# Second-block mixing with finer hand-overs and ScalarE making half of the scan's bounded differences

## The chip, the cores and the metric

The kernel runs on one core of one Trainium2 chip, as one launch. Its engines are TensorE (PE, with its weight loads shown apart as PEld), VectorE (DVE), ScalarE (ACT), GpSimd (POOL) and the queue of SyncE (SP), which here only issues DMAs. The metric is the device time of one execution in microseconds, the median of the runs.

## The reference, cut to what matters

All is fp32, 256 tokens (two tiles of 128) of width 1024. A first block has two layers with ffn halves, a state-space scan (layer 0) and pooling (layer 1). A second block has two layers; each mixes (attention, short convolution, spatial gating) and then sums 128 chosen experts per token.

```python
# first block, scan of one chunk of 128 tokens, 32 heads, two directions
seg = a_cum[:, :, :, None] - a_cum[:, :, None, :]
Lmat = jnp.exp(jnp.where(mask, seg, -jnp.inf))
cb = jnp.einsum('bclgn,bcsgn->bclsg', Cc, Bc)
y_diag = jnp.einsum('bclsg,bclsge,bcsgep->bclgep', cb, Lmat, xdt)
y_off = jnp.einsum('bclgn,bcgepn,bclge->bclgep', Cc, h_in, jnp.exp(a_cum))

# second block, one layer
h = rms_norm(x, norm1_g) * (1 + sc1) + sh1
proj = h @ w_in                                # 1024 x 2048
y_attn, y_conv, y_sgu = ...                    # 512, 256 and 256 columns
merged = concatenate([rms_norm(y_attn, ga), rms_norm(y_conv, gc), rms_norm(y_sgu, gs)])
x = x + g1 * (merged @ w_out)                  # 1024 x 1024
h2 = rms_norm(x, norm2_g) * (1 + sc2) + sh2
x = x + g2 * peer_ffn(h2, ...)                 # 8 heads x 16 experts per token; each: dot with a row, gelu, times gate, times a second row, summed
```

## The kernel before, in words

Each engine has a stream of its own, written by hand, and they meet through semaphores. The order of the first block is: `ffn0`, `ffn1`, the scan's projections, the scan, its output projection, `ffn2`, `ffn3`, pooling, `ffn4`. Weights come through a ring of six 1 MB tiles.

**The scan.** 32 batches, each a chunk, a direction and four heads. TensorE makes the running sums of a batch for all positions (`running_sums`, into PSUM bank `BC_BANK[b % 3]`) two batches ahead, and then the outputs of the batch (`outputs`). VectorE (`segments`) subtracts each position's own sum and bounds the difference at zero, four instructions of 128 columns; ScalarE (`exponents`) makes `exp` of the sums (`eoff`) and of the bounded differences (`decay`), 512 columns each; VectorE (`weights`) multiplies by the masked products `cbm`, one batch behind; GpSimd multiplies `eoff`. Between batches VectorE also has `skip`, `weigh_dt`, `gated`, `group_scale` and `group_norm`, and TensorE three `group_sums`; ScalarE has two square roots, each with a change of its table to and back. `decay`, `eoff` and the banks are rings of three, freed by `y_done`, and by `seg_ready` and `expbc_ready`.

**The second block.** Four units `g` (layer, token tile). A unit first mixes and selects its experts, then its 128 picks come: GpSimd gathers a pick's two rows of 1024 for all 128 tokens by an indirect DMA of 1 MB into one of eight slots (`rows`), VectorE makes the dot (L2294), ScalarE gelu, gate and a diagonal matrix (`diag`), and TensorE adds the second row through that diagonal (L625), or VectorE for some picks (L1587). The mixing of unit `g` is a generator (`mix`) on each engine; `mix_slot(g, step)` says before which pick of unit `g - 1` a step is done. For unit 0 all slots of the mixing lie before the first pick, so there it runs by itself, and the picks of unit 0 begin when its first 32 expert numbers (`eidx`) are there. The gathers are in order on GpSimd's queue; the weight tiles of the second block (8 of `w_in`, 4 of `w_out`, 8 of `peer_wq`, 4 small `keys`) come through a ring of four on SP's queue, each reloaded when `weights2_used` says so.

In `mix`, before the change: ScalarE squares and roots (`square_norm`), makes `gd` (eight diagonals of the residual gate `g1` or `g2`), scales the tokens into `xs`. TensorE broadcasts the gate (ones times `gd`, banks 2 and 3), turns `xs` (banks 4 and 5), and ScalarE evicts the eight blocks with norm scale and shift into `u2`, then the gate into `g_b`. Only when all eight blocks are there (`u2_ready`) does TensorE begin `columns`, a tile of 256 columns as eight fp32 matmuls. After attention ScalarE squares the three groups of `merged` (512, 256, 256), one root each, VectorE one reciprocal, ScalarE scales the groups, TensorE turns eight blocks, ScalarE evicts them into `mergedT`, and then four `columns` of `w_out` follow. VectorE waits for all four, multiplies by the gate and adds, 1024 columns each. The second norm goes as the first, and its blocks are turned once more into `h2tok`.

Nearly all instructions of an engine have the line of a helper: L625 is every matmul, L628 every transpose, L1132 every ScalarE activation, L1584 `tensor_tensor`, L1587 `scalar_tensor_tensor`, L1590 `tensor_scalar`, L2427 the gather. `u2` shows as `u`, `decay` as `arena`, `eoff` as `hT` and `xres` as `x_tok`.

## Time and profile before

| what | value |
|---|---|
| median of 3 runs | 3089.16 us (3086.47 to 3093.55) |
| profiled execution | 3088.0 us, span 3085.1 us |
| PE, DVE, ACT, POOL busy | 84%, 71%, 35%, 24% of the span |
| DMA | 977.06 MB, mean 317 GB/s |
| scan | about 691 to 785 us |
| unit 0's mixing | about 1484 to 1615 us |
| picks of four units | 1615 to 3085 us |

A busy share is an average over stages with different limits, so the stages are looked at apart: which wait ends last in each. PE and PEld overlap, and a busy PE isn't PE at its peak. Granted clock 1.00 is 2.4 GHz of TensorE, 0.50 is 1.2 GHz. An instruction's mean is its own duration; the next of the same engine can start before it ends. One profiled execution gives all durations.

### The profile page before, as it was taken

Reading aid. Unit: us, or ns where it says so; the run is one execution under the profiler, and the core shown is the slowest. Engines: PE = TensorE matmul, PEld = TensorE weight load, DVE = VectorE, ACT = ScalarE, POOL = GpSimd, SP = SyncE. Lnnn points to the kernel's source line nnn. Section 1 sums busy time; section 2 is a strip of 40 time slices with the busy share of each in tenths; the row PEclk is TensorE's granted clock in tenths of the full one; section 3 lists DMA queues with packets and bytes.
Section 4 is the critical chain, followed back from the end, with each engine's and each line's share of the span. In section 5 each row is a group of like instructions: output and inputs, shape, how many; then the busy total and the mean of one; then the engine's idle time right before and its main releaser. Section 6 shows DMA issues by size and latency. Waiting matters only on the chain.

```text
span 3085.1 us, 37413 instructions
## 1 busy us (share of the span) xinstructions
PE 2604.5 (84%) x13854; PEld 1978.6 (64%) x13854; DVE 2183.9 (71%) x3896; ACT 1074.0 (35%) x2248; POOL 738.9 (24%) x683
## 2 busy tenths in 40 slices
PE   7999999998999999899876788767786788876656
PEld 5999998886899899899762355324553245532212
DVE  6886866649368878678228766797667966689675
ACT  4434333324243434433322333223432244332221
POOL 0000000005000000000004434344433443344553
PEclk9999999999999999999888898999899998999878
DMA  7766963330369689389449999999999999999997
GB/s 311 266 231 239 369 241 140 112 134 2 130 237 363 258 316 365 138 329 360 161 146 420 409 418 409 420 419 419 421 421 420 411 407 400 420 422 421 421 419 325
DMA packets 137015, 977.06 MB, mean 317 GB/s; under 512 B 15517, under 2 KB 15525, under 8 KB 18992
## 3 DMA queue, kind: packets, MB, share of 16 engines
q0 software_dynamic: 91088, 661.23, 52.7%
q1 hardware_dynamic: 44496, 308.06, 26.2%
q10 hardware_dynamic: 1296, 6.04, 0.5%
q8 instruction: 75, 1.23, 0.2%
q14 instruction: 60, 0.49, 0.0%
HBM read 974.21 MB, written 1.06 MB: 316 GB/s over the span
## 4 chain that ended last, share of the span: by engine, by line
PE 50%; DMA 24%; DVE 14%; issue 5%; ACT 5%; POOL 1%; DVEq 0%; ACTq 0%; POOLq 0%
PE psum L625 49%; DMA rows<-in_peer,eidx 23%; DVE rows L2294 3%; DVE yacc L1587 2%; DVE arena L1732 1%; PE psum L628 1%; ACT L1132 1%; DVE wlow L1584 1%; DVE arena L1584 1%; POOL rows L2427 1%; DVE rep L2083 1%; DVE arena L1590 1%; ACT u L1132 0%; ACT dots L1132 0%; DMA arena<-in_ada_t 0%
## 5 line engine op out<-in xcount | busy, mean ns | idle before, releaser
L625 PE MATMUL psum<-rows,diag 128*128 128x512 f32 x1440 | 791.3, 692 | 347.4 <-ACT diag L1132 340.9
L2294 DVE CUSTOM_DVE_ANT_0 rows<-rows,h2tok 128x1024 f32<-128x1024 f32 x512 | 626.7, 1225 | 334.1 <-DMA rows<-in_peer,eidx 326.2
L2427 POOL DMA_INDIRECT rows<-in_peer,eidx x512 | 618.2, 1207 | 959.6 <-PE psum L625 560.7
L625 PEld LDWEIGHTS psum<-rows,diag 128*128 128x128 f32 x1440 | 292.5, 216 | 777.9 <-ACT diag L1132 493.8
L625 PE MATMUL psum<-u_hi,whigh 128*128 128x256 f32 x1760 | 505.3, 287 | 20.9 <-DVE u_lo L1587 18.1
L625 PE MATMUL psum<-u_lo,whigh 128*128 128x256 f32 x1760 | 501.6, 285 | 0.0
L625 PE MATMUL psum<-u_hi,wlow 128*128 128x256 f32 x1760 | 501.3, 285 | 0.0
L1584 DVE TENSOR_TENSOR wlow<-wring,whigh 128x2048 fp32r<-128x2048 f32 x165 | 377.1, 2289 | 120.9 <-ACT whigh L1132 115.3
L1132 ACT ACTIVATE whigh<-wring 128x2048 fp32r<-128x2048 f32 x165 | 314.1, 1908 | 173.0 <-PE psum L625 132.5
L1132 ACT ACTIVATE dots<-dots 128x2 f32<-128x2 f32 x256 | 52.2, 204 | 891.7 <-DVE dots L2294 891.5
L625 PEld LDWEIGHTS psum<-u_hi,whigh 128*128 128x128 f32 x1760 | 340.8, 194 | 24.1 <-issue 19.3
L625 PEld LDWEIGHTS psum<-u_lo,whigh 128*128 128x128 f32 x1760 | 341.6, 194 | 0.0
L625 PEld LDWEIGHTS psum<-u_hi,wlow 128*128 128x128 f32 x1760 | 341.5, 194 | 0.0
L2388 POOL DMA_DIRECT2D arena<-in_ada_t x112 | 59.5, 532 | 965.5 <-DVE stage L1732 667.4
L1732 DVE CUSTOM_DVE_ANT_0 arena<-arena 128x1024 f32<-128x1024 f32 x224 | 265.5, 1220 | 10.3 <-DMA arena<-in_ada_t 10.3
L625 PE MATMUL psum<-hid_hi,whigh 128*128 128x256 f32 x880 | 250.0, 284 | 3.9 <-DVE wlow L1584 3.9
L625 PE MATMUL psum<-wring,u 128*128 128x256 f32 x1056 | 246.3, 389 | 6.8 <-ACT u L1132 6.8
L625 PE MATMUL psum<-hid_lo,whigh 128*128 128x256 f32 x880 | 249.8, 284 | 0.0
L625 PE MATMUL psum<-hid_hi,wlow 128*128 128x256 f32 x880 | 249.7, 284 | 0.0
L625 PEld LDWEIGHTS psum<-wring,u 128*128 128x128 f32 x1056 | 206.3, 196 | 61.6 <-issue 25.1
L625 PE MATMUL psum<-arena,wring 128*128 128x256 f32 (+1 forms) x912 | 200.5, 380 | 0.0
L1587 DVE SCALAR_TENSOR_TENSOR yacc<-rows,dots,yacc 128x1024 f32<-128x1024 f32 x148 | 189.7, 1282 | 0.0
(274 smaller groups left out, 3231.1 us busy)
## 6 DMA issues: line engine op xcount, KB each, us to landing
arena<-in_ada_t POOLq DMA_DIRECT2D x116, 1024.0 KB, 7.5
wring<-in_ffn_w_gate SPq DMA_DIRECT2D x55, 1024.0 KB, 6.3
wring<-in_ffn_w_up SPq DMA_DIRECT2D x55, 1024.0 KB, 7.1
wring<-in_ffn_w_down SPq DMA_DIRECT2D x55, 1024.0 KB, 6.5
wring<-in_w_in SPq DMA_DIRECT2D x32, 1024.0 KB
wring<-in_peer_wq SPq DMA_DIRECT2D x32, 1024.0 KB
wring<-in_ssd_w_in SPq DMA_DIRECT2D x30, 1024.0 KB, 4.8
wring<-in_w_out SPq DMA_DIRECT2D x16, 1024.0 KB
```

Source lines behind the costliest of these rows:

```text
L625: return nc.tensor.matmul(out, lhsT, rhs, start=start, stop=stop, skip_group_check=shared)
L628: return nc.tensor.transpose(out, in_, ident[0:in_.shape[0], 0:in_.shape[0]])
L1132: return nc.scalar.activation(out, in_, fn, **kw)
L1584: return v.tensor_tensor(out, a, b, op)
L1587: return v.scalar_tensor_tensor(out=out, in0=a, scalar=s, in1=b, op0=op0, op1=op1)
L1590: return v.tensor_scalar(out, a, s1, s2, op0, op1) if op1 is not None else v.tensor_scalar(out, a, s1, None, op0)
L1732: ins = v.tensor_tensor_reduce(out=w, in0=w, in1=crow[:, ADA_VECTOR[n], :], scale=1.0, scalar=0.0, op0=ALU.mult, op1=ALU.add, accum_out=st ...
L2083: ins = v.match_replace(out=spare[:, i, :], in_to_replace=vals[:, i, 0:8], in_values=src[:, i, :], imm_value=-3.0e38)
L2294: v.tensor_tensor_reduce(out=rows[:, n % SLOTS, 0:D], in0=rows[:, n % SLOTS, 0:D], in1=h2tok[:, t, :], scale=1.0, scalar=0.0, op0=ALU.mult ...
L2388: pool.dma_start(aring[:, a % ADA_RING].rearrange("p a b -> p (a b)"), A["ada_t"][it + 4 * (group + a)]) \
L2427: pool.indirect_dma_start(out=rows[:, n % SLOTS, :], out_offset=None, in_=A[f"peer{u // 2}"], in_offset=bass.IndirectOffsetOnAxis(ap=eidx[ ...
```

## The change

It has two parts, in the same functions of the kernel.

- **Scan.** `segments` on VectorE makes the bounded differences of two of a batch's four heads. For the other two ScalarE's `exponents` makes `Relu(-sum + own sum)` from PSUM, which is the bounded difference with its sign turned, and takes its exponent with scale -1. So `decay`'s exponent is two instructions of 256 columns, with a wait for ScalarE's own Relu between.
- **Mixing, all four units.** `xs` is scaled in two halves, each with its count of `xs_ready`. `gd` is made after the eight blocks of `u2`, and the gate's broadcast goes behind tile 1 of `w_in`, into banks 4 and 5, with its own semaphore (`gd_ready`) and `tok_done` back. Each block of `u2` counts, and the first tile and the second transposes wait block by block. In the merge, groups 1 and 2 are squared, rooted, inverted, scaled and turned as soon as they are there (slots 24 to 29), group 0 after attention; the blocks are evicted in `MERGED_ORDER`, each counting, and the first tile of `w_out` takes them in that order. The residual is added in four quarters, each as its tile is done, and the second norm's squares are made in two parts (768 and 256 columns). `qksq_ready` goes.

```diff
+MERGED_ORDER = (4, 5, 6, 7, 0, 1, 2, 3)
...
             def turn_norm(m):
-                pe.wait_ge(xs_ready, m + 1)
                 for k in range(KB):
+                    if k % 4 == 0:
+                        pe.wait_ge(xs_ready, 2 * m + k // 4 + 1)
                     ins = transpose(bank(4 + k // 4, (k % 4) * P, P), xs[:, k * P:(k + 1) * P])
                 ins.then_inc(xs_turned, 1)
-            def columns(n, b, src):
+            def columns(n, b, src, blocks=range(KB), ready=None, value=0):
                 w = tile2(n).rearrange("p (k n) -> p k n", k=KB)
-                for k in range(KB):
-                    ins = mm(bank(b, 0, 256), src[:, k, :], w[:, k, :], k == 0, k == KB - 1)
+                for i, k in enumerate(blocks):
+                    if ready is not None:
+                        pe.wait_ge(ready, value + i + 1)
+                    ins = mm(bank(b, 0, 256), src[:, k, :], w[:, k, :], i == 0, i == KB - 1)
                 ins.then_inc(weights2_used, 1)
...
                 yield mix_slot(g, 2)
-                pe.wait_ge(xs_ready, 2 * g + 1)
-                for k in range(KB):
-                    mm(bank(2 + k // 4, (k % 4) * P, P), ones[:], gd[:, k, :], True, True)
                 turn_norm(2 * g)
                 for i in range(8):
                     yield mix_slot(g, 4 + 2 * i)
-                    if i == 0:
-                        pe.wait_ge(u2_ready, 2 * g + 1)
-                    if i == 2:
-                        pe.wait_ge(gb_ready, g + 1)
                     if i >= 4:
                         pe.wait_ge(win_evicted, 8 * g + i - 3)
-                    columns(len(SECOND) * g + i, i % 4, u2)
+                    if i == 0:
+                        columns(len(SECOND) * g, 0, u2, ready=u2_ready, value=16 * g)
+                    else:
+                        columns(len(SECOND) * g + i, i % 4, u2)
+                    if i == 1:
+                        pe.wait_ge(gd_ready, g + 1)
+                        for k in range(KB):
+                            ins = mm(bank(4 + k // 4, (k % 4) * P, P), ones[:], gd[:, k, :], True, True)
+                        ins.then_inc(tok_done, 1)
                     if i == 6:
                         yield mix_slot(g, 17)
                         pe.wait_ge(qk_ready, g + 1)
+                        pe.wait_ge(gb_ready, g + 1)
...
-                yield mix_slot(g, 33)
-                pe.wait_ge(mscaled_ready, g + 1)
-                for k in range(KB):
-                    ins = transpose(bank(4 + k // 4, (k % 4) * P, P), merged[:, k * P:(k + 1) * P])
-                ins.then_inc(merged_turned, 1)
+                for half in (1, 0):
+                    yield mix_slot(g, 29 if half else 33)
+                    pe.wait_ge(mscaled_ready, 2 * g + 2 - half)
+                    for k in range(4):
+                        ins = transpose(bank(5 - half, k * P, P), merged[:, (4 * half + k) * P:(4 * half + k + 1) * P])
+                    ins.then_inc(merged_turned, 1)
                 for i in range(4):
                     yield mix_slot(g, 35 + 2 * i)
-                    if i == 0:
-                        pe.wait_ge(mergedT_ready, g + 1)
-                    columns(len(SECOND) * g + 8 + i, i, mergedT)
+                    columns(len(SECOND) * g + 8 + i, i, mergedT, MERGED_ORDER, mergedT_ready if i == 0 else None, 8 * g)
                 yield mix_slot(g, 45)
                 turn_norm(2 * g + 1)
                 yield mix_slot(g, 47)
-                pe.wait_ge(u2_ready, 2 * g + 2)
                 for k in range(KB):
+                    pe.wait_ge(u2_ready, 16 * g + 8 + k + 1)
                     ins = transpose(bank(2 + k // 4, (k % 4) * P, P), u2[:, k, :])
...
                 act.wait_ge(seg_ready, b + 1)
+                c, jb, d = (b // 2) % 2, b // 4, b % 2
+                for i in (2, 3):
+                    h = 32 * d + 4 * jb + i
+                    ins = f(decay[:, b % 3, i * P:(i + 1) * P], bank(BC_BANK[b % 3], i * P, P), ACT.Relu, scale=-1.0, bias=acum[:, c, h:h + 1])
+                tick(ins)
                 f(eoff[:, b % 3, :], bank(BC_BANK[b % 3]), ACT.Exp).then_inc(expbc_ready, 1)
-                f(decay[:, b % 3, :], decay[:, b % 3, :], ACT.Exp).then_inc(expseg_ready, 1)
+                f(decay[:, b % 3, 0:2 * P], decay[:, b % 3, 0:2 * P], ACT.Exp)
+                settle()
+                f(decay[:, b % 3, 2 * P:4 * P], decay[:, b % 3, 2 * P:4 * P], ACT.Exp, scale=-1.0).then_inc(expseg_ready, 1)
...
             def scale_norm(m, t):
                 act.wait_ge(n_rstd, m + 1)
-                f(xs[:], xres[:, t, :], ACT.Identity, scale=nstat[:, 2:3]).then_inc(xs_ready, 1)
+                for half in (slice(0, 512), slice(512, D)):
+                    f(xs[:, half], xres[:, t, half], ACT.Identity, scale=nstat[:, 2:3]).then_inc(xs_ready, 1)
             def evict_norm(m):
                 act.wait_ge(xs_turned, m + 1)
                 for k in range(KB):
-                    ins = f(u2[:, k, :], bank(4 + k // 4, (k % 4) * P, P), ACT.Identity,
-                            scale=gscale[:, 9 + m, k:k + 1], bias=NORM2_SHIFT[m][:, k:k + 1])
-                ins.then_inc(u2_ready, 1)
+                    f(u2[:, k, :], bank(4 + k // 4, (k % 4) * P, P), ACT.Identity,
+                      scale=gscale[:, 9 + m, k:k + 1], bias=NORM2_SHIFT[m][:, k:k + 1]).then_inc(u2_ready, 1)
...
                 act.wait_ge(mods_ready, 5 + l)
-                for k in range(KB):
-                    c = (40 if t else 16) + k
-                    f(gd[:, k, :], ident[:], ACT.Identity, scale=mod2[:, l, c:c + 1])
                 yield mix_slot(g, 1)
                 scale_norm(2 * g, t)
                 yield mix_slot(g, 3)
                 evict_norm(2 * g)
-                f(g_b[:, t, :], psum[:, 2:4, :].rearrange("p a b -> p (a b)"), ACT.Identity).then_inc(gb_ready, 1)
+                for k in range(KB):
+                    c = (40 if t else 16) + k
+                    ins = f(gd[:, k, :], ident[:], ACT.Identity, scale=mod2[:, l, c:c + 1])
+                ins.then_inc(gd_ready, 1)
                 for p, i in enumerate(W_IN_ORDER):
                     yield mix_slot(g, 5 + 2 * p)
+                    if p == 2:
+                        act.wait_ge(tok_done, 22 + g)
+                        f(g_b[:, t, :], psum[:, 4:6, :].rearrange("p a b -> p (a b)"), ACT.Identity).then_inc(gb_ready, 1)
...
-                yield mix_slot(g, 31)
-                act.wait_ge(merged_ready, g + 1)
-                for i, (a, b) in enumerate(((0, 512), (512, 768), (768, 1024))):
+                act.wait_ge(merged_ready, 2 * g + 1)
+                for i, (a, b) in ((1, (512, 768)), (2, (768, 1024))):
                     ins = f(osq[:, a:b], merged[:, a:b], ACT.Square, accum_out=ostat[:, i:i + 1])
                 tick(ins)
                 settle()
-                f(ostat[:, 0:1], ostat[:, 0:1], ACT.Sqrt, scale=1.0 / 512, bias=eps[:, 0:1])
                 f(ostat[:, 1:3], ostat[:, 1:3], ACT.Sqrt, scale=1.0 / 256, bias=eps[:, 0:1]).then_inc(ostd_ready, 1)
-                yield mix_slot(g, 32)
-                act.wait_ge(orstd_ready, g + 1)
-                for i, (a, b) in enumerate(((0, 512), (512, 768), (768, 1024))):
+                yield mix_slot(g, 29)
+                act.wait_ge(orstd_ready, 2 * g + 1)
+                for i, (a, b) in ((1, (512, 768)), (2, (768, 1024))):
                     ins = f(merged[:, a:b], merged[:, a:b], ACT.Identity, scale=ostat[:, i:i + 1])
                 ins.then_inc(mscaled_ready, 1)
+                yield mix_slot(g, 31)
+                act.wait_ge(merged_ready, 2 * g + 2)
+                tick(f(osq[:, 0:512], merged[:, 0:512], ACT.Square, accum_out=ostat[:, 0:1]))
+                settle()
+                f(ostat[:, 0:1], ostat[:, 0:1], ACT.Sqrt, scale=1.0 / 512, bias=eps[:, 0:1]).then_inc(ostd_ready, 1)
+                yield mix_slot(g, 32)
+                act.wait_ge(orstd_ready, 2 * g + 2)
+                f(merged[:, 0:512], merged[:, 0:512], ACT.Identity, scale=ostat[:, 0:1]).then_inc(mscaled_ready, 1)
                 yield mix_slot(g, 34)
-                act.wait_ge(merged_turned, g + 1)
-                for k in range(KB):
-                    ins = f(mergedT[:, k, :], bank(4 + k // 4, (k % 4) * P, P), ACT.Identity, scale=col("out_g", 8 * l + k))
-                ins.then_inc(mergedT_ready, 1)
+                for i, k in enumerate(MERGED_ORDER):
+                    if i % 4 == 0:
+                        act.wait_ge(merged_turned, 2 * g + i // 4 + 1)
+                    f(mergedT[:, k, :], bank(4 + i // 4, (i % 4) * P, P), ACT.Identity, scale=col("out_g", 8 * l + k)).then_inc(mergedT_ready, 1)
                 yield mix_slot(g, 43)
-                act.wait_ge(mixed_in, g + 1)
-                square_norm(2 * g + 1, t)
+                act.wait_ge(mixed_in, 4 * g + 3)
+                tick(f(xs[:, 0:768], xres[:, t, 0:768], ACT.Square, accum_out=nstat[:, 0:1]))
+                settle()
+                tick(f(nstat[:, 3:4], nstat[:, 0:1], ACT.Identity, scale=1.0 / D, bias=eps[:, 0:1]))
+                act.wait_ge(mixed_in, 4 * g + 4)
+                tick(f(xs[:, 768:D], xres[:, t, 768:D], ACT.Square, accum_out=nstat[:, 1:2]))
+                settle()
+                f(nstat[:, 1:2], nstat[:, 1:2], ACT.Sqrt, scale=1.0 / D, bias=nstat[:, 3:4]).then_inc(n_std, 1)
...
-                for i in range(4):
+                for i in range(2):
...
-                tick(tt(merged[:, 512:768], proj[:, 768:1024], bank(4, 0, 256), ALU.mult))
+                settle()
+                tt(merged[:, 512:768], proj[:, 768:1024], bank(4, 0, 256), ALU.mult).then_inc(merged_ready, 1)
                 yield mix_slot(g, 27)
                 dve.wait_ge(pexp_ready, g + 1)
                 tick(tt(den, rsum, es, ALU.add))
                 settle()
                 tick(v.reciprocal(den, den))
                 settle()
+                yield mix_slot(g, 29)
+                dve.wait_ge(ostd_ready, 2 * g + 1)
+                v.reciprocal(ostat[:, 1:3], ostat[:, 1:3]).then_inc(orstd_ready, 1)
...
-                dve.wait_ge(ostd_ready, g + 1)
-                v.reciprocal(ostat[:, 0:3], ostat[:, 0:3]).then_inc(orstd_ready, 1)
+                dve.wait_ge(ostd_ready, 2 * g + 2)
+                v.reciprocal(ostat[:, 0:1], ostat[:, 0:1]).then_inc(orstd_ready, 1)
                 yield mix_slot(g, 42)
-                dve.wait_ge(weights2_used, len(SECOND) * g + 12)
                 dve.wait_ge(gb_ready, 2 * l + 1)
-                tick(tt(xadd[:, :].rearrange("p (a b) -> p a b", a=4), psum[:, 0:4, 0:256], g_b[:, 0, :].rearrange("p (a b) -> p a b", a=4), ALU.mult))
-                settle()
-                tt(xres[:, t, :], xres[:, t, :], xadd[:], ALU.add).then_inc(mixed_in, 1)
+                for i in range(4):
+                    part = slice(256 * i, 256 * i + 256)
+                    dve.wait_ge(weights2_used, len(SECOND) * g + 9 + i)
+                    tick(tt(xadd[:, part], bank(i, 0, 256), g_b[:, 0, part], ALU.mult))
+                    settle()
+                    tt(xres[:, t, part], xres[:, t, part], xadd[:, part], ALU.add).then_inc(mixed_in, 1)
```

## Rows read from the trace of the kernel before

**Rows 1.** The page's chain that ended last, by engine.

```profile
PE 50%; DMA 24%; DVE 14%; issue 5%; ACT 5%; POOL 1%; DVEq 0%; ACTq 0%; POOLq 0%
```

**Rows 2.** Windows: us, busy per engine (instructions), PEclk, DMA share, GB/s.

```profile
1620.00:3040.00 1420.00, 1059.13 (x2928) 547.51 (x2928) 1059.30 (x2247) 451.81 (x1487) 605.10 (x501) 0.89 1.01 417
1748.00:1784.00 36.00, 33.28 (x116) 21.23 (x117) 18.64 (x29) 14.35 (x47) 12.98 (x11) 0.91 0.98 395
1840.00:1900.00 60.00, 48.78 (x181) 30.76 (x180) 39.38 (x58) 28.20 (x77) 26.72 (x23) 0.88 1.00 402
```

**Rows 3.** DMA queues' total, 1616 to 3085 us.

```profile
DMA packets 84559, 604.85 MB, mean 412 GB/s; under 512 B 9392, under 2 KB 9392, under 8 KB 11312
```

**Rows 4.** Chain in order of time (start, us, what), at the first gather.

```profile
1614.88 0.19 DVE eidx L2147
```

**Rows 5.** The same chain, unit 0's first norm.

```profile
1486.13 2.33 ACT gd L1132 x8
1488.47 1.05 ACT xs L1132
...
1489.56 3.79 PE psum L625 x16
...
1495.09 2.92 ACT u L1132 x8
...
1498.05 26.13 PE psum L625 x112
```

**Rows 6.** The same chain, unit 0 from the merge to the first query tile.

```profile
1548.25 1.53 ACT osq L1132 x6
...
1554.10 2.19 ACT mergedT L1132 x8
...
1556.33 16.09 PE psum L625 x64
...
1572.45 1.24 DVE xadd L1584
...
1577.94 1.98 PE psum L628 x8
...
1584.87 8.38 PE psum L625 x32
```

**Rows 7.** Timeline of ACT: start, us, engine, line, out<-in, count [idle before].

```profile
1503.49 0.38 ACT L1132 ACTIVATE proj<-psum 128x256 f32<-128x256 f32 x1 [4.58 <-PE psum L625]
...
1544.95 0.20 ACT L1132 ACTIVATE warm<-eps 128x1 f32<-128x1 f32 x1
```

**Rows 8.** Windows as in rows 2, in the scan and at tile 8.

```profile
761.00:767.00 6.00, 3.89 (x26) 3.37 (x28) 6.00 (x12) 1.24 (x4) 2.58 (x1) 0.72 0.00 0
1556.00:1558.00 2.00, 1.67 (x4) 1.40 (x5) 0.00 (x0) 0.28 (x2) 0.00 (x0) 0.50 0.00 0
```

**Rows 9.** Timeline of PE: first outputs of batches 3, 13, 14, 20, 28.

```profile
701.71 0.45 PE L625 MATMUL psum<-arena 128*64 128x128 f32 x4 [1.60 <-DVE arena L1584]
...
727.74 0.45 PE L625 MATMUL psum<-arena 128*64 128x128 f32 x4
...
729.91 0.45 PE L625 MATMUL psum<-arena 128*64 128x128 f32 x4
...
745.32 0.45 PE L625 MATMUL psum<-arena 128*64 128x128 f32 x4
...
775.10 0.51 PE L625 MATMUL psum<-arena 128*64 128x128 f32 x4 [2.01 <-DVE arena L1584]
```

**Rows 10.** Groups by form, 693 to 784 us: busy, mean ns | idle, releaser.

```profile
L1590 DVE TENSOR_SCALAR arena<-psum,arena 128x128 f32<-128x128 f32 x120 | 33.6, 342 | 8.8 <-PE psum L625 8.5
...
L625 PE MATMUL psum<-arena 128*64 128x128 f32 x240 | 27.3, 298 | 17.8 <-DVE arena L1584 17.6
L1132 ACT ACTIVATE arena<-arena 128x512 f32<-128x512 f32 x30 | 18.7, 623 | 0.0
...
L1132 ACT ACT_TABLE_LOAD x4 | 5.1, 1283 | 3.3 <-DVE arena L1590 3.3
```

More of the change, by code:

```diff
@@ L415, in program @@
         gb_ready = sem("gb_ready")
+        gd_ready = sem("gd_ready")
         win_evicted = sem("win_evicted")
-        qksq_ready = sem("qksq_ready")
         vc_ready = sem("vc_ready")
@@ L1466, in mix @@
                         act.wait_ge(win_evicted, 8 * g + 3)
-                        f(qsq[:], proj[:, 0:640], ACT.Square).then_inc(qksq_ready, 1)
+                        f(qsq[:], proj[:, 0:640], ACT.Square)
                     if p == 4:
```

1 line of the change is left out of this document (removed).

## The prediction

> **What bounds the kernel now.** I read the chain of work that ended last first: half of it is TensorE, a quarter is DMA of gathered rows [rows 1]. So the kernel has two regimes, and the same saved microsecond is worth different things in them. Next the busy times by stage [rows 2]: from 1620 us to 3040 us the DMA engines are busy all the time and move 417 GB/s, while no compute engine is full. That stage moves 604.85 MB [rows 3], 512 gathers of 1.05 MB (2.5 us each at that rate) and the weights of units 1 to 3. Its length is bytes over rate; only its beginning can move. It begins when the first expert numbers are ready, at 1614.88 + 0.19 = 1615.1 us [rows 4]. All before it is compute bound, so a microsecond taken there ends the kernel a microsecond sooner. From this follows how the change must be read: the four-unit `mix` edits count once, in unit 0 (1484 to 1615 us, nothing else runs beside it), and the same edits in units 1 to 3 lie under saturated DMA. The scan edit lies at 690 to 785 us and counts in full, since the ffn stages behind it are paced by TensorE.
>
> **Unit 0, first norm.** The reader is to see in [rows 5] a pure relay: ACT makes `gd` until 1488.46, scales `xs` (1.05), PE broadcasts the gate (16 matmuls from 1489.56), transposes, ACT evicts eight blocks (2.92), and only then does column tile 0 start, at 1498.05. After: `gd` no longer stands ahead of the scaling, so that starts at 1486.45. Half of it is 0.6 us, PE starts at 1487.1, its eight transposes take 2.0 (1.98 for the same eight at 1577.94, [rows 6]), the first block is evicted in 2.92/8 = 0.37, and column tile 0 starts at about 1489.6: 8.4 us earlier. The gate broadcast doesn't vanish; it now stands on PE behind tile 1. Broadcast and transposes took 5.5 us together (1489.56 to 1495.06), so it took 3.5, at the low clock of a start after idling; behind two tiles of matmuls the clock is likely 1.0 (2.4 GHz), so I take 2.0 (bounds 1.7 and 3.5). Net 6.4. That broadcast now makes PE wait for `gd_ready`; queued behind it are tiles 2 to 7. ACT makes `gd` (2.33) directly behind the evictions, by about 1494.9, while PE is in tiles 0 and 1 until 1497, so this wait costs nothing.
>
> **Unit 0, merge.** In [rows 6] the squares begin at 1548.25, after the attention output, for all three groups; root, reciprocal and scaling follow, then eight transposes, eight evictions (2.19), and the w_out tiles start at 1556.33. After: the two groups that don't come from attention are squared, rooted, scaled and turned while PE does the value matmuls (ACT is free from 1545.15 [rows 7]; the two squares, their root, the reciprocal and the two scalings come to about 2.2, so it is through before 1548.25). What stays: square of 512 columns with its accumulator read 0.75, root 0.3, reciprocal 0.2, scaling 0.7, four transposes 1.0: 1548.25 + 3.0 = 1551.3. The first four evictions go beside those transposes, the others beside tile 8, which takes the blocks in that order. Gain 5.0.
>
> **Unit 0, residual and second norm.** From the end of the w_out tiles (1572.43) to the first query tile (1584.87) there are 12.4 us [rows 6]: two full-width DVE operations (1.24 each), square and root, scaling, transposes, evictions and the transposes of `h2tok`, of the sizes of [rows 5]. After: only the last quarter is left behind the last tile (two operations of about 0.4: a quarter of 1.24 and a little), square of 256 columns 0.5, root 0.3, reciprocal 0.25, half a scaling 0.65, transposes 2.05, evictions 2.95 with the second transposes beside them and 0.3 behind: 7.9. Gain 4.5.
>
> **Clock.** The first column tile after such a relay runs at granted clock 0.50 [rows 8]. Tile 0 took 5.4 us (1498.05 to its eviction at 1503.49, [rows 7]) out of 26.13 for seven [rows 5], so the others 3.45 each; four w_out tiles took 16.09 [rows 6], which is three of 3.45 and a first of 5.7. The relays shrink and PE's work begins earlier ahead of the tile, so some of these 1.9, 2.3 and, for the query tiles, 1.4 us goes. Bounds: none of it and all of it, 5.6; I take 2.1, since the relays stay longer than half of what they were. Sum for unit 0: 6.4 + 5.0 + 4.5 + 2.1 = 18.0, with bounds 14.5 and 21.8. Weights don't intervene: no DMA stands in this part of the chain, and later tiles are requested by the very tiles that now come earlier.
>
> **The scan.** Per batch PE does running sums and outputs; where nothing waits that is 2.17 us (727.74 to 729.91, [rows 9]). From 701.71 to 745.32 there are 17 batches in 43.6 us against 38.7 (17 x 2.17 and 1.8 of group sums), from 745.32 to 775.10 eight in 29.8 against 19.2. The rest is PE waiting for DVE, 17.8 us in all [rows 10]. DVE gives up two of four bounded differences, 2 x 0.28 = 0.56 us a batch [rows 10]. In the first stretch that brings DVE under PE's 2.17 except at the two batches with `gated`, where I keep 0.5 each: 4.9 - 1.0 = 3.9 gained. In the second DVE stays the bound, because reciprocals and norms stand between the batches: four batches give 2.2. But ScalarE's part grows: two Relu of 128 columns from PSUM with a bias column. No row shows one; the nearest are the evictions with a scale column (2.19/8 = 0.27) and with two columns (2.92/8 = 0.37) [rows 5, 6], so 0.55 to 0.75 for two; I take 0.6. Splitting the second exponent adds 0.2. From the end of the DVE part to the exponents' end takes now 1.2, then 2.0; with DVE's part shorter by 0.56 the products can begin 0.2 later than before. In the steady stretches DVE comes to them only a batch later, so that hides it; at batch 24, where the exponents wait for a root's two table loads, it costs 0.6. Gain 3.9 + 2.2 - 0.6 = 5.5, and I take 5.0 for seams (bounds: 1 lost, if the ACT path decides everywhere; 11 gained, if the PE clock, which falls in the second stretch, holds too). ScalarE's time per batch, now two exponents of at most 0.62 [rows 10], becomes at most 0.6 + 1.24 + 0.2 = 2.0, under 2.17.
>
> By the Trainium skill, ScalarE: Activation LUTs, section Rules for kernel authors, `relu`, `min` and `add` belong on VectorE and not on ScalarE. The rows agree that ScalarE is no faster at it (0.3 against 0.28); were that what decides, the scan would gain nothing and the total would be 17.0. What decides here is which engine PE waits for [rows 10], so I don't follow it.
>
> **Units 1 to 3.** Here the finer waits cannot shorten bytes over rate. DMA falls below 421 GB/s only in patches, such as 402 over 1840 to 1900 us (2.7 us lost) and 395 over 1748 to 1784 (2.2 lost) [rows 2]. The first is the merge: ScalarE works through squares, root and scalings between picks. The change puts a second root there, so one more pair of table loads, 2 x 1.28 [rows 10], per unit, with row releases queued behind it; eight row slots (20 us of DMA) cover most. The other patch may ease, since the gate broadcast moves out of the block ahead of tile 0. Bounds: 6 gained, 9 lost; I take 1 lost.
>
> **Sum.** 18.0 + 5.0 - 1.0 = 22.0. The profiled execution took 3088.0 us (span 3085.1), so 3066.0; it lies 1.2 under the median 3089.16 and inside the runs' 7 us, so I forecast 3066 for the median too.
>
> **Rivals.** (a) Half of it: the scan gains nothing because ScalarE's longer relay becomes the wait, and unit 0 keeps the slow clock; 14.5 - 2 gained, 3075. For it speaks that ScalarE's latency grows by more than DVE's work falls; against it, that DVE now reaches the products late anyway. (b) More: the clock comes back in unit 0 and in the scan's second stretch and the patches ease; 3051. The clock at 0.72 in parts of that stretch [rows 8] makes it possible. (c) Slower: the Relu isn't in the exponents' table. Then each batch has two table loads on ScalarE, 2.57 us more [rows 10], ScalarE needs 2.0 + 2.6 = 4.6 a batch. The 25 batches from 701.71 to 775.10 [rows 9] take 73.4 us now, 2.9 each, and would take 115; for all 32 it is 53 lost, with 17 gained elsewhere 3124. It decides from about 2.9 + 17/32 = 3.5 us of ScalarE per batch, so one load would not do it. Against it: Identity, Square and Exp alternate in the scan with four loads in all, each at a root or a silu [rows 10]. The Trainium skill, in the same page, section Table sets, says that relu is a filler in every set; by that rule no load comes. (d) It doesn't do what it says: the split waits in units 1 to 3 hold picks so long that the gather stage stretches by what unit 0 won, 18 us or 6 a unit, over twice the present loss there: 3084.
>
> **How the numbers follow.** Forecast 0.68 (own range 3058 to 3074), (a) 0.14, (b) 0.08, (c) 0.03, (d) 0.07. About 0.2% (6 us) is what a measurement of this kernel tells from no change. Range 3051 to 3080: it takes in (a) and most of (b) and leaves (c), (d) out. Faster 0.91; same 0.05, most of (d); slower 0.04, (c) and the rest.
>
> **What would show it.** Right: column tile 0 starts about 8 us sooner after the root than now, tile 8 about 3 us after the merge, the first query tile about 8 us after the last w_out tile; the first expert numbers at 1592; from there to the end again 1470 us; PE's wait for DVE in the scan well under 17.8, with loads still four; DMA at 420 GB/s. Wrong: the stage from first gather to end longer than 1475 (then the patches grew), or ACT named as what PE or DVE waits for in the scan.

## The result and the profile after

| kernel | median | runs | profiled span |
|---|---|---|---|
| before | 3089.22 us | 4, 3086.47 to 3093.55 | 3085.1 us |
| after | 3068.81 us | 4, 3066.01 to 3073.64 | 3064.1 us |

The ratio is 0.9937, 95% interval 0.9925 to 0.9948: 20.4 us faster. The two spans differ by 21.0 us, and all but 0.1 of it is ahead of the first gather. The span falls into three pieces: up to the first square of unit 0's mixing 4.15 us were gained (1481.22 before, 1477.07 after), in unit 0's mixing, from that square to the first expert numbers, 16.76 us (133.85, now 117.09), in the rest 0.09 us (1470.03, now 1469.94).

First the page's chain by engine, against [rows 1], and the window that answers to the first of [rows 2]; the gather stage is unchanged (416 GB/s, 417 before).

```profile
PE 48%; DMA 27%; DVE 13%; issue 5%; ACT 4%; POOL 1%; DVEq 0%; ACTq 0%; POOLq 0%
```

```profile
1620.00:3040.00 1420.00, 1057.31 (x2939) 545.04 (x2938) 1060.05 (x2237) 463.32 (x1512) 612.43 (x502) 0.90 1.01 416
```

The chain in order of time in unit 0 of the kernel after (start, us, what), which answers to [rows 4], [rows 5] and [rows 6]:

```profile
1482.55 0.73 ACT xs L1139
...
1483.32 1.98 PE psum L631 x8
...
1485.33 0.47 ACT u L1139
...
1485.93 29.17 PE psum L628 x128
...
1531.52 1.11 PE psum L631 x8
...
1538.23 0.73 ACT osq L1139 x2
...
1539.51 0.73 ACT merged L1139
...
1540.29 1.12 PE psum L631 x4
1541.40 14.75 PE psum L628 x64
...
1556.18 0.43 DVE xadd L1613
...
1559.00 1.28 PE psum L631 x8
...
1560.31 0.47 ACT u L1139
...
1560.82 2.92 PE psum L631 x8
1563.74 8.60 PE psum L628 x32
...
1593.97 0.19 DVE eidx L2176
```

The reader is to see that `gd` is gone from the relay, that one eviction (`u`, 0.47) stands where eight did, and that one group of the merge (`osq` 0.73, `merged` 0.73) is left on the chain. The 128 matmuls from 1485.93 are the 112 of [rows 5] and the 16 of the gate broadcast, which now stand among them.

The scan, groups by form from 693 to 784 us (busy, mean ns, idle before and its releaser), against [rows 10]:

```profile
L1613 DVE TENSOR_TENSOR arena<-arena 128x512 f32<-128x512 f32 x42 | 39.3, 953 | 6.2 <-ACT arena L1139 6.2
L628 PE MATMUL psum<-arena 128*64 128x128 f32 x248 | 27.9, 295 | 17.7 <-DVE arena L1613 17.6
...
L1139 ACT ACTIVATE arena<-psum,arena 128x128 f32<-128x128 f32 x60 | 18.7, 365 | 30.6 <-DVE arena L1619 26.0 <-PE psum L628 4.5
L1619 DVE TENSOR_SCALAR arena<-psum,arena 128x128 f32<-128x128 f32 x60 | 18.1, 342 | 9.0 <-PE psum L628 8.9
...
L1139 ACT ACT_TABLE_LOAD x4 | 5.1, 1283 | 0.1
```

Half of VectorE's differences are gone (60 of 120, 15.5 us of busy time), ScalarE's Relu takes 0.365 us, there are still four table loads. Yet PE's wait for DVE is 17.7 us as before [rows 10]. The first outputs of batches 3, 20, 28 and 29, against [rows 9]:

```profile
701.19 0.45 PE L628 MATMUL psum<-arena 128*64 128x128 f32 x4 [1.09 <-DVE arena L1613]
...
745.12 0.45 PE L628 MATMUL psum<-arena 128*64 128x128 f32 x4 [0.57 <-DVE arena L1613]
...
773.44 0.45 PE L628 MATMUL psum<-arena 128*64 128x128 f32 x4 [1.50 <-DVE arena L1613]
777.33 0.45 PE L628 MATMUL psum<-arena 128*64 128x128 f32 x4
```

Batches 3 to 20 take 43.9 us, before 43.6: nothing gained where 3.9 was forecast. Batches 20 to 28 take 28.3, before 29.8. Where the lost 3.9 went is what the second half of the experiments is about.

### The profile page after: what moved, and what is told of

Its sections match the earlier page's. It is cut to its first block, busy times and chain, and to the rows that moved or that the text cites. A ratio compares the mean times of both kernels' runs of the same rounds, so it can differ in the third digit from the quotient of the medians.

```text
span 3064.1 us, 37504 instructions
## 1 busy us (share of the span) xinstructions
PE 2593.8 (85%) x13854; PEld 1970.7 (64%) x13854; DVE 2177.8 (71%) x3860; ACT 1107.0 (36%) x2370; POOL 734.6 (24%) x683
## 4 chain that ended last, share of the span: by engine, by line
PE 48%; DMA 27%; DVE 13%; issue 5%; ACT 4%; POOL 1%; DVEq 0%; ACTq 0%; POOLq 0%
PE psum L628 47%; DMA rows<-in_peer,eidx 27%; DVE rows L2328 2%; DVE yacc L1616 2%; DVE arena L1761 2%; DVE wlow L1613 1%; DVE arena L1613 1%; PE psum L631 1%; ACT L1139 1%; POOL rows L2461 1%; DVE rep L2112 1%; ACT dots L1139 0%; ACT diag L1139 0%; ACT xs L1139 0%; ACT prob L1139 0%
## 5 line engine op out<-in xcount | busy, mean ns | idle before, releaser
L628 PE MATMUL psum<-u_hi,whigh 128*128 128x256 f32 x1760 | 506.4, 288 | 21.8 <-DVE u_lo L1616 18.1
```

Of the source, the lines that this page charges most:

```text
L628: return nc.tensor.matmul(out, lhsT, rhs, start=start, stop=stop, skip_group_check=shared)
```

## Experiments: which part brings what

**scan_only**: before, with the scan of after (the hunk of ScalarE's differences and VectorE's `range(2)`).

```diff
-                for i in range(4):
+                for i in range(2):
...
+                    ins = f(decay[:, b % 3, i * P:(i + 1) * P], bank(BC_BANK[b % 3], i * P, P), ACT.Relu, scale=-1.0, bias=acum[:, c, h:h + 1])
```

> The kernel before with the scan edit alone. Theory (what is won is won ahead of the first gather and nowhere else): the scan's last batch starts 3.3 us sooner, as in the changed kernel's trace, the first gather 3 to 4 us sooner, the stage from first gather to end stays 1470 us; time 3 to 4 us down (0.1%). Rival (the prediction's 5.0): 5 us down.

3088.05 us (11 runs) against 3088.41: ratio 0.9997, interval 0.9988 to 1.0006. That is 0.9 us less where 3 to 4 were expected, and can't be told from nothing; the interval ends at 3.7. In its trace batches 3 to 20 take 43.9 us and unit 0's mixing starts 3.1 us sooner than in before (1478.08), its span is 2.8 shorter (3082.3).

Even these 3 us aren't all the edit's. Seven kernels of this document have the scan of before: before itself, mix_only, unit0_only, units123_only, norms_alone, merge_alone and residual_alone. First outputs to first outputs, by PE's timeline:

| scan | kernels | 3 to 20 | 20 to 28 | 28 to 31 |
|---|---|---|---|---|
| before | five of the seven | 43.6 us | 29.8 | 9.4 |
| before | units123_only, merge_alone | 43.6 | 29.8 | 7.8 |
| after | after, scan_only | 43.9 | 28.3 | 7.8 |

The first two columns repeat within 0.02 us, so there the edit is worth -0.3 and 1.5, in sum 1.2 us. In the last one two kernels have the 7.8 us without the edit. The windows behind batch 28 of before, units123_only and after tell why (columns as in [rows 2], PEclk is the last but two):

```profile
775.00:781.00 6.00, 5.90 (x40) 4.99 (x41) 2.49 (x10) 1.80 (x4) 2.72 (x2) 0.72 0.00 0
```

```profile
778.00:784.00 6.00, 5.26 (x56) 4.52 (x53) 3.61 (x11) 2.46 (x5) 2.94 (x3) 1.00 0.01 3
```

```profile
775.00:781.00 6.00, 4.62 (x47) 3.84 (x46) 3.21 (x5) 4.05 (x10) 2.97 (x3) 1.00 0.01 3
```

So these 1.6 us are where the low clock falls, and it isn't shown that the edit moves it.

**mix_only**: after, with the scan of before.

```diff
-                for i in (2, 3):
-                    ins = f(decay[:, b % 3, i * P:(i + 1) * P], bank(BC_BANK[b % 3], i * P, P), ACT.Relu, scale=-1.0, bias=acum[:, c, h:h + 1])
...
+                f(decay[:, b % 3, :], decay[:, b % 3, :], ACT.Exp).then_inc(expseg_ready, 1)
```

> The changed kernel with the scan as before. Theory: unit 0's mixing 16.8 us shorter (from the first ScalarE square of the second block to the first expert numbers, 133.9 to 117.1 us), gather stage 1470 us, time 16 to 18 us down (0.55%). Rival (the two parts help each other, for example by the clock): less than 15 us down, and scan_only and mix_only together not the 20.4 us of the whole.

3070.52 us (5 runs): ratio 0.9948, 0.9935 to 0.9962, 16 us gained. Unit 0's mixing takes 117.27 us. This part carries the change. The two parts timed alone multiply to 0.9945, the whole is 0.9937; that lies inside mix_only's interval, so whether the parts help each other (the rival of this run) isn't settled.

**unit0_only** and **units123_only**: the scan of before, and the new mixing in some units, the old one in the others: each new step stands under a test of the unit's number, and the old code in its other branch.

```diff
+NORM_FINE, MERGE_FINE, RES_FINE = (0,), (0,), (0,)                     # unit0_only
+NORM_FINE, MERGE_FINE, RES_FINE = (1, 2, 3), (1, 2, 3), (1, 2, 3)      # units123_only
```

> Scan as before, and the finer hand-overs in unit 0 alone; units 1 to 3 mix as before. Theory: as mix_only, 16 to 18 us down, within 3 us of it. Rival (units 1 to 3 pay for their second root and their waits, the record's bounds 6 gained to 9 lost): 5 us or more away from mix_only.

> Scan as before, unit 0 mixes as before, and the finer hand-overs only in units 1 to 3, where the picks of the unit before run beside them. Theory (bytes over rate sets that stage): within 3 us of the kernel before. Rival (relays in any unit count): 10 us or more down; or, if the second root holds row releases, 3 to 9 us up.

unit0_only: 3074.5 us, ratio 0.996 (0.9946 to 0.9973), unit 0's mixing 119.54 us. units123_only: 3086.25 us, ratio 0.9994 (0.9985 to 1.0003), unit 0's mixing 134.29 us, gather stage 1469.09. What counts is unit 0. Units 1 to 3 bring 1.9 us by units123_only and 3.7 by the difference of mix_only and unit0_only (3 was the most that I expected; 2.3 of it are in unit 0's own mixing in the two profiles, where the code is the same). Neither is above the measurement's own width, but a loss of 18, 6 a unit, as the rival (d) had it, is excluded, and of the 1 us of loss that I took nothing is seen (the interval of units123_only ends at 0.9 lost). Profiles can't say more: between kernels with the new mixing in all units, so with the same gather code, the stage's length ranges from 1469.6 to 1472.7 us, and 1475.4 in after_nopool below, whose output is another. They also show that unit 0's new code takes 117.1 to 119.5 us, with the same instructions: columns 29.03, w_out tiles 16.36 us in unit0_only, 27.81 and 15.32 in mix_only.

**norms_alone**, **merge_alone**, **residual_alone**: the scan of before and one of the three parts of the mixing.

```diff
+NORM_FINE, MERGE_FINE, RES_FINE = (0, 1, 2, 3), (), ()   # norms_alone
+NORM_FINE, MERGE_FINE, RES_FINE = (), (0, 1, 2, 3), ()   # merge_alone
+NORM_FINE, MERGE_FINE, RES_FINE = (), (), (0, 1, 2, 3)   # residual_alone
```

> Scan of before; of the second block's mixing only the norms' finer hand-overs (halves of the scaled rows, each evicted block announced by itself, the gain's broadcast behind the second tile) in all units; merge and residual as before. Theory (the terms add up): unit 0's mixing, 133.9 us before and 117.3 with all three parts, takes 124 to 126 us (first norm 6.4 to 8, second norm some 2). Rival (a part gives up its gain when it stands alone, since the low-clock stretch then falls on other products): over 127 us.

> Scan of before; of the mixing only the merge in halves (the two quarter-width parts squared, scaled and turned ahead of the attention part). Theory (the terms add up): unit 0's mixing 128 to 129.5 us (133.9 less 4.9). Rival (clock falls elsewhere): outside 127 to 130.5 us.

> Scan of before; of the mixing only the residual in quarters with each quarter's square following it. Theory (the terms add up): unit 0's mixing 130.5 to 132 us (133.9 less 2 to 3). Rival: no change, 133.5 us or more, since the last quarter's chain is as long as the whole row's was.

Each was run once, for its trace. Unit 0's mixing took 125.25, 127.63 and 130.02 us: 8.6, 6.2 and 3.8 less than the 133.85 of before. The first lies inside what was expected, the other two 0.4 and 0.5 us under its lower end. The sum is 18.65 us, and the three together gain 16.6 (mix_only): the terms add up but for 2.1 us. The relays themselves are the same alone and together (the merge's, from the last value product to the first w_out tile, is 3.95 us alone, 3.96 in after, 8.87 before). The 2.1 lies in the matmuls behind the relays, whose length goes with the granted clock, and nearly all of it in the query tiles' 32: 8.38 us before, 7.75, 7.95 and 8.01 in the three alone, but 8.89 in mix_only. Summed against before that is 1.43 gained alone and 0.51 lost together, 1.9 of the 2.1. Why the low clock reaches them in mix_only isn't shown. Chain of merge_alone, and windows of after (columns as in [rows 2]):

```profile
1550.04 15.08 PE psum L629 x64
```

```profile
1485.00:1491.00 6.00, 5.36 (x14) 4.12 (x13) 1.23 (x1) 5.21 (x16) 0.00 (x0) 0.50 0.04 18
1491.00:1493.00 2.00, 2.00 (x8) 1.67 (x8) 0.00 (x0) 0.37 (x1) 0.00 (x0) 0.76 0.00 0
1540.00:1542.00 2.00, 1.72 (x6) 1.59 (x7) 0.00 (x0) 1.82 (x8) 0.00 (x0) 0.50 0.00 0
1542.00:1544.00 2.00, 2.00 (x8) 1.67 (x7) 0.00 (x0) 0.58 (x3) 0.00 (x0) 0.71 0.00 0
```

w_out's 64 matmuls took 16.09 us before [rows 6], 15.08 here, 14.75 in after, 15.32 in mix_only and 16.36 in unit0_only, where the clock is back at other moments. Tile 0, which PE reaches in after 2.6 us behind its restart, is worked on at 0.50 for over five microseconds: 29.17 less 1.78 of broadcast less six tiles of 3.45 are 6.7 us for it, 5.4 before. But this doesn't come with the new relay: norms_alone and mix_only have it too, their columns took 27.81 us, which leaves 5.3 for tile 0; and scan_only and units123_only have the old relay, and there the 112 matmuls took 27.31 and 27.34 us instead of 26.13, so tile 0 took 6.6. Which matmuls get the low clock changes between kernels that have the same code there.

## Experiments: where the scan's 3.9 us went

Three theories. A: ScalarE's longer relay makes the products late. B: VectorE and GpSimd get in each other's way: VectorE's 128x512 products grew from 0.76 to 0.95 us on average over the scan, while GpSimd multiplies (its own mean fell from 1.64 to 1.38). C: PE waits for GpSimd's product itself, under VectorE's name. The means are from the groups by form of 693 to 784 us; two of before and GpSimd's of after (VectorE's of after is shown above):

```profile
L2398 POOL TENSOR_TENSOR hT<-hT,arena 128x512 f32<-128x512 f32 x30 | 49.0, 1636 | 46.4 <-ACT hT L1132 46.4
...
L1584 DVE TENSOR_TENSOR arena<-arena 128x512 f32<-128x512 f32 x42 | 31.3, 761 | 2.4 <-ACT arena L1132 2.4
```

```profile
L2432 POOL TENSOR_TENSOR hT<-hT,arena 128x512 f32<-128x512 f32 x30 | 41.5, 1384 | 50.6 <-ACT hT L1139 50.6
```

**before_nopool** and **after_nopool**: GpSimd's product `eoff` times the state rows cut from 512 columns to 4 in both kernels. The rest of that term isn't computed, so the output isn't the reference's. One execution each.

```diff
-                g.tensor_tensor(e, e, xbc[:, 20 + jb // 2, c * P:(c + 1) * P].unsqueeze(1).to_broadcast([P, 4, P]), ALU.mult) \
+                g.tensor_tensor(e[:, :, 0:1], e[:, :, 0:1], xbc[:, 20 + jb // 2, c * P:c * P + 1].unsqueeze(1).to_broadcast([P, 4, 1]), ALU.mult) \
```

> The changed kernel with GpSimd's product of eoff in the scan cut from 512 to 4 columns, so the scan's state term is left undone for the others. From batch 3 to batch 20 the kernel before took 43.6 us and the changed one 43.9, where 38.7 is TensorE's own. Theory (VectorE's three-operand products, 0.68 us alone and up to 1.35 while GpSimd multiplies, took back what the two differences gave): VectorE's 128x512 products fall from a mean of 0.95 to about 0.68 us and the 17 batches to 39 to 40.5 us. Rival (ScalarE's longer relay is the wait): products may be quicker, but the 17 batches stay at 43 us or more, with VectorE waiting for ScalarE.

> The kernel before with the same cut of GpSimd's product. Theory: VectorE's products fall from a mean of 0.76 to 0.68 us; the 17 batches take 41.5 to 43 us, since four differences a batch still hold VectorE; so with GpSimd out of the way the change is worth 2 to 3.5 us there, near the predicted 3.9. Rival: the 17 batches take the same in both, within 0.5 us.

Spans 3059.5 and 3076.8 us. From the first outputs of batch 3, by PE's timeline:

| kernel | 3 to 20 | 3 to 31 | VectorE's products, 701 to 746 |
|---|---|---|---|
| before | 43.61 us | 82.79 us | 18.1 us |
| after | 43.93 | 80.03 | 25.4 |
| before_nopool | 43.45 | 77.69 | 17.9 |
| after_nopool | 39.50 | 72.46 | 18.0 |

The last column is from the groups by form of 701 to 746 us; the rows of before, after, before_nopool and after_nopool, in that order:

```profile
L2398 POOL TENSOR_TENSOR hT<-hT,arena 128x512 f32<-128x512 f32 x18 | 31.1, 1725 | 16.7 <-ACT hT L1132 16.7
L1584 DVE TENSOR_TENSOR arena<-arena 128x512 f32<-128x512 f32 x27 | 18.1, 691 | 0.0
```

```profile
L1613 DVE TENSOR_TENSOR arena<-arena 128x512 f32<-128x512 f32 x27 | 25.4, 959 | 0.2 <-ACT arena L1139 0.2
L2432 POOL TENSOR_TENSOR hT<-hT,arena 128x512 f32<-128x512 f32 x18 | 25.2, 1398 | 22.9 <-ACT hT L1139 22.9
```

```profile
L1584 DVE TENSOR_TENSOR arena<-arena 128x512 f32<-128x512 f32 x27 | 17.9, 684 | 0.0
```

```profile
L1613 DVE TENSOR_TENSOR arena<-arena 128x512 f32<-128x512 f32 x27 | 18.0, 684 | 0.0
```

With GpSimd out of the way the edit gains 43.45 - 39.50 = 3.95 us in the first stretch, which is the 3.9 forecast, and 77.69 - 72.46 = 5.2 from batch 3 to batch 31, where the forecast took 5.0. With GpSimd there it gains -0.3 and 2.8. My expectation for before_nopool was short: 41.5 to 43 us, so a gain of 2 to 3.5. Before, the same cut changes the first stretch by only 0.2 us: VectorE's products weren't slowed there, GpSimd's were (31.1 us for 18). Behind batch 20 it isn't so: there the cut takes 4.9 us off before, of which 1.3 are VectorE's products (8.8 us for 11, now 7.5) and a part is the clock (0.91 over 746 to 784 us, now 1.00). After, they cost VectorE 7.3 us more in the first stretch and GpSimd 5.9 less.

So theory A falls: ScalarE's chain is the same in after_nopool, where VectorE waits for it 5.8 us (693 to 780 us; 6.2 in after, 693 to 784), and the gain is whole; and in the first stretch VectorE waits for ScalarE 0.2 us in after, as its row above shows. Theory C would fit this experiment as well as B, since the cut also makes GpSimd's product short. The trace of after decides: at each of batches 3 to 20 at which PE waits, its outputs begin 0.05 or 0.06 us behind the end of VectorE's product and at least 0.60 behind the end of GpSimd's. For batch 20 it can be read off the rows shown: GpSimd's product of 742.04 ended at 743.39, PE began at 745.12.

One meeting in each kernel's timeline (start, us; x2 are two products in a row), first before, then after:

```profile
742.31 1.28 DVE L1584 TENSOR_TENSOR arena<-arena 128x512 f32<-128x512 f32 x2
742.66 2.06 POOL L2398 TENSOR_TENSOR hT<-hT,arena 128x512 f32<-128x512 f32 x1 [0.70 <-ACT hT L1132]
```

```profile
740.44 1.27 POOL L2432 TENSOR_TENSOR hT<-hT,arena 128x512 f32<-128x512 f32 x1 [2.66 <-ACT hT L1139]
...
741.00 2.94 DVE L1613 TENSOR_TENSOR arena<-arena 128x512 f32<-128x512 f32 x2
742.04 1.35 POOL L2432 TENSOR_TENSOR hT<-hT,arena 128x512 f32<-128x512 f32 x1 [0.34 <-ACT hT L1139]
```

Before, VectorE came first: its two products took their 1.28 us and GpSimd's 1.27 us of work began about when they were over (2.06 = 0.79 of waiting and 1.27). After, GpSimd was in its product when VectorE came: that stays at 1.27, GpSimd's next one (742.04) gets in between VectorE's two, and the pair takes 2.94. What decides in these two meetings is who is in its product already. The Trainium skill, SBUF — State Buffer, section SBUF: two separate sides, has it as a rule: VectorE with two inputs in SBUF and GpSimd reading SBUF take the same port pair, whoever starts first keeps it for a whole instruction, and the other stands. These rows agree that one stands while the other works, with 0.79 and 2.94 - 1.28 = 1.66 us of standing. They don't show why GpSimd stood for both of VectorE's products before and got in between them after, which a rule for one instruction leaves open.

**one_head**: after, with one difference of four on ScalarE instead of two (and the second exponent split into 384 and 128 columns).

```diff
-                for i in (2, 3):
+                for i in (3,):
...
-                for i in range(2):
+                for i in range(3):
```

> The changed kernel with one of four differences made by ScalarE instead of two. Theory: VectorE has 0.28 us a batch more than in the changed kernel and ScalarE a Relu less; the products still start early enough to meet GpSimd's, so the 17 batches take 43.5 to 44.5 us and the time is the changed kernel's within 2 us. Rival (ScalarE's relay costs): 42 to 43 us and 1 us faster than the changed kernel's 0.9937.

3069.63 us (4 runs), ratio 0.9936 (0.992 to 0.9951), the same as after. Batches 3 to 20 take 42.0 us, less than with two (43.9) though VectorE does more. I had expected 43.5 to 44.5; 42.0 is what the rival named, that ScalarE's relay costs, though its 1 us in the total isn't there. The rival's cause doesn't stand, since after_nopool has the whole relay and is quicker still; what fell is VectorE's products, 20.3 us, not 25.4. Batches 20 to 28 take 29.1 against 28.3. So the length fits B, by fewer slowed products than I thought, and speaks against any account by the number of operations alone.

**eoff_first**: after, with the exponent of the sums ahead of ScalarE's two differences, so that GpSimd's product begins earlier; PE's wait before the sums' bank is used again goes to the later of the two signals.

```diff
+                f(eoff[:, b % 3, :], bank(BC_BANK[b % 3]), ACT.Exp).then_inc(expbc_ready, 1)
                 for i in (2, 3):
...
-                f(eoff[:, b % 3, :], bank(BC_BANK[b % 3]), ACT.Exp).then_inc(expbc_ready, 1)
```

> The changed kernel with ScalarE's exponent of the sums ahead of the two Relu (TensorE then waits for the second exponent before it fills the bank). GpSimd's product starts 0.5 us sooner in each batch. Theory: it then meets less of VectorE's products (mean under 0.90 instead of 0.95 us), the 17 batches take 1 to 2 us less than 43.9, the time 1 to 3 us less than the changed kernel's. Rival (it meets others instead, as many): 17 batches within 0.5 us of 43.9.

3068.15 us (5 runs), ratio 0.9930 (0.9916 to 0.9943). Batch 31's first outputs come at 779.20 us, 2.0 sooner than in after, but batches 3 to 20 take 43.7 us, where 1 to 2 less than 43.9 were expected: an earlier product of GpSimd doesn't give the stretch back, which again speaks against C. VectorE's 27 products of 512 columns did fall, to 21.7 us, but its two of 1024 rose from 2.4 to 4.6: other products are met, as the rival had it. Unit 0's mixing happened to take 118.28 us (117.09 in after), which hides most of the 2.0 in the total.

**mixed_heads**: eoff_first, with one difference on ScalarE in batches 0 to 19 and two from batch 20.

```diff
-                for i in (2, 3):
+                m = 3 if b < 20 else 2
+                for i in range(m, 4):
...
-                for i in range(2):
+                for i in range(3 if b < 20 else 2):
```

> Changed kernel with the exponent of the sums ahead of ScalarE's two differences, and with only one difference per batch on ScalarE in batches 0 to 19 (two from batch 20). Theory (VectorE's 128x512 products are slowed while GpSimd multiplies; fewer meet where ScalarE takes one head): the stretch from batch 3 to batch 20 takes about 42.0 us as with one head (43.7 to 43.9 with two), the rest of the scan stays as where the sums come first; outputs of batch 31 near 777.5 us (781.2 in the changed kernel, 779.2 with the sums first), whole about 3066.5 us. Rival (the stretch is set by the length of ScalarE's own chain, and the sums first have already taken what there was): batch 31 at 779 us or later, whole 3068 us.

3068.95 us (5 runs), ratio 0.9941 (0.9928 to 0.9955): no better. Batches 3 to 20 take 44.6 us where I expected 42.0. VectorE's 128x512 products are indeed little slowed there (19.0 us), but the two of 1024 columns, in the batches with `gated`, are hit as in eoff_first. Against one_head that costs 0.8 us at each of the two, batches 9 to 10 and 17 to 18. The other 1.1 of the 2.6 us lie in batches 18 to 20 (5.86 us against 4.78), where the granted clock is 0.50 from 742 to 744 us in mixed_heads and 1.00 in one_head. The gated batch's meeting in the timelines of one_head and of mixed_heads (three products in a row, the middle one of 1024 columns):

```profile
714.55 2.42 DVE L1613 TENSOR_TENSOR arena<-arena 128x512 f32<-128x512 f32 x3
...
715.17 2.93 POOL L2432 TENSOR_TENSOR hT<-hT,arena 128x512 f32<-128x512 f32 x1 [0.76 <-ACT hT L1139]
```

```profile
713.27 3.50 DVE L1614 TENSOR_TENSOR arena<-arena 128x512 f32<-128x512 f32 x3
...
713.62 1.46 POOL L2433 TENSOR_TENSOR hT<-hT,arena 128x512 f32<-128x512 f32 x1 [0.58 <-ACT hT L1139]
```

In mixed_heads GpSimd's product comes 0.35 us behind VectorE's first one, gets in ahead of the long one and is through in 1.46; in one_head it comes 0.62 behind and stands until all three are over. In before it came 0.36 behind (715.02 against 714.66) and stood too, 3.19 us. So the distance of the starts alone doesn't tell who gets in between; that stays open. The step of my expectation that failed is that fewer meetings mean a shorter stretch: it is also which product is hit, and here the clock fell as well. Moving ScalarE's steps about can't be expected to win the 3.9 by design. What could, an order fixed by a wait of GpSimd for VectorE's products, wasn't tried. None of the variants can be told from after.

## Why the prediction was right, and where it wasn't

**Total.** Forecast 22.0 us of gain, 3066.0; measured 20.4, 3068.81, and 21.0 between the profiled spans. The range held it, the case was the likeliest. The total is nearer than its terms: the scan's edit gave 1.2 us that repeat where 5.0 were forecast, and 1.6 of clock in the scan, 0.9 between the stages and a 1 us loss that didn't come made up for part of it. That is luck, and not the mechanism.

**First norm.** Forecast 8.4 for the relay less 2.0 for the broadcast. The way from the first square to tile 0 fell from 16.83 to 8.86 us, by 8.0; the broadcast took 1.8 in its new place. 6.2 for 6.4. The wait for `gd_ready` cost nothing, as worked out.

**Merge.** 4.9 for 5.0. **Residual and second norm**: 12.44 us became 7.59, 4.85 for 4.5.

**Clock.** 2.1 forecast, about 0.7 measured: tile 8's stretch won 1.3 and the probabilities' transposes 0.9 (1.98 to 1.11), but tile 0 lost 1.3 and the query tiles 0.2. By the same four pieces mix_only won 0.4 and unit0_only lost 1.2, with the same mixing in unit 0. The step that failed is "PE's work begins earlier ahead of the tile, so some of these goes". I had counted only gains, and as if the relays' length set them; the runs show the low clock on other matmuls from kernel to kernel, tile 0 at 5.3 to 6.7 us behind the new relay and at 5.4 to 6.6 behind the old one. So the 0.7 isn't shown to be the change's, and 1.98 to 1.11 was seen without it too (before_nopool).

**Scan.** 5.0 forecast, 3.3 measured at batch 31 (784.50 to 781.22), and it is made of other terms: 0.5 up to batch 3 (in kernels with the scan of before that moment ranges from 701.6 to 704.4, so it tells nothing), -0.3 instead of 3.9 for batches 3 to 20, 1.5 instead of 1.6 for 20 to 28, and 1.6 behind that, where PE's clock held 1.00 from 775 to 781 us (0.72 before), which two kernels with the scan of before show too. The failing step is "that brings DVE under PE's 2.17": it took VectorE's products at the length that they had in this stretch while VectorE was first at the meetings with GpSimd (0.69 us on average). Without GpSimd's product the step gives 3.95. I should have asked why GpSimd's product took 1.64 us on average and 1.27 at best: the two engines already met, and in that stretch only their order kept VectorE from paying. So PE's wait for DVE, which was to fall well under 17.8 us, stayed at 17.7. Two other terms held: two Relu take 0.62 us of ScalarE where 0.6 was taken (0.365 each, overlapping), and there is no fifth table load. Of the signs of being wrong one did come: ACT isn't named as what PE waits for, but it is for DVE's products, 6.2 us where it was 2.4 in before. It wasn't what cost the 3.9, since after_nopool has 5.8 of it.

**Behind the scan.** 0.9 us of the 4.15 lie between batch 31 and the second block, where nothing was changed; that stretch ranges from 693.7 us (unit0_only, units123_only) to 697.7 (residual_alone) over the kernels of this case, with the same code in it. So 0.9 is nothing that can be told.

**Units 1 to 3.** 1.0 lost was forecast; 1.9 to 3.7 gained were timed, below what can be told, and 0.1 in the profile. That the row slots cover the new root, as the prediction had it, is only argued.

**Rivals.** (a) the scan gains nothing in its first stretch, as it says, but not by ScalarE's relay. (b) its clock came back in the scan, 1.6 us of it, but so it did in two kernels with the scan of before. (c) four loads, as before. (d) the gather stage is 1469.94 us for 1470.03.

The sum by the measured terms: 6.2 + 4.9 + 4.85 + 0.7 = 16.65 of the 16.76 in unit 0, 3.3 in the scan, 0.9 unexplained, 0.1 in the gathers: 21.0. Of these, the three relays' 16.0 and the scan's 1.2 are what the runs tie to the change.

## What to carry to other kernels

Ahead of a stage that is bytes over rate, a relay between engines is worth its full length, and its length without the clock could be priced from the rows of before (15.9 forecast, 16.0 measured): count what is left behind the last producer, not what is made finer. Work taken from the engine that everyone waits for isn't a gain before you have looked who else is in memory with it: if a third engine's operation shows a mean well above its minimum, the two already meet, and an earlier start can turn round who waits. And don't credit a clock that came back to an edit before other kernels with the same code in that stretch have been looked at: 1.6 us in the scan and 1.3 at tile 0 came and went without the edit.

## What the runs showed of the hardware

VectorE's 128x512 product of two SBUF operands takes 0.68 us alone (after_nopool) and up to 1.81 us when GpSimd is already in its own (after); GpSimd's takes 1.27 us alone and up to 3.19 behind VectorE (before). The recorded duration contains the waiting, so busy time grows without more work: 18.1 to 25.4 us for the same 27 products. TensorE's low clock falls in different places of the same code: unit 0's mixing, with the same instructions, took 117.1 to 119.5 us, and the scan's batches 28 to 31 took 9.4 us in five kernels and 7.8 in two, at a granted clock of 0.72 and 1.00 over their first six us. Which product gets in between two of the other engine isn't settled by the starts alone (0.35 and 0.36 us behind, with opposite ends).
